# Scan factors of two mixers on VectorE instead of GpSimd, and one weight chunk of the third mixer split earlier

## The chip, the cores and the metric

The kernel runs on one core of a Trainium2 chip. The core has TensorE (matrix products into PSUM banks), VectorE, ScalarE and GpSimd (elementwise work) and SyncE, which only issues loads here. The engines run their own instruction streams in order and meet at semaphores. The metric is the device time of one execution, in microseconds; lower is better.

## The reference, cut to what matters

The model is two blocks in a row on 256 tokens of width 1024, all in float32. The first block (attention, a Fourier mix and a convolutional feed-forward, two layers) is not touched by the change. The second block has two layers, which this text calls the second and the third mixer. Both contain a gated scan over time in chunks of 32 tokens, forwards and backwards:

```python
def _chunk_gated_scan(q, k, v, log_g):
    ...
    b = jnp.cumsum(log_g, axis=2)
    ref = b[:, :, CHUNK // 2 - 1:CHUNK // 2]
    s = jnp.einsum('bnthk,bnshk->bnhts', q * jnp.exp(b - ref), k * jnp.exp(ref - b))
    s = jnp.where(np.tril(np.ones((CHUNK, CHUNK), bool)), s, 0.0)
    o_intra = jnp.einsum('bnhts,bnshv->bnthv', s, v)
    b_last = b[:, :, -1]
    q_dec = q * jnp.exp(b)
    k_dec = k * jnp.exp(b_last[:, :, None] - b)
    ...

def _mixer_c(h, w_in, lower_bounds, layer_idx, norm_gain, w_out):
    proj = jnp.einsum('bsd,df->bsf', h, w_in)
    q, f_f, f_b, i, gate = _split(proj, (C_WIDTH,) * 5)
    ...
    f = lb + (1.0 - lb) * jax.nn.sigmoid(z)        # forget: k = 1 - f, g = log f, per direction
    o = bidirectional_gated_scan(silu(q) * scale, k_f, g_f, k_b, g_b, i)
    y = _head_rmsnorm(o, norm_gain) * jax.nn.silu(gate)
    return y @ w_out
```

## The kernel before, in words

**Products.** Weights come in chunks of 1 MB (128 x 2048 floats) that SyncE loads into a ring of two slots. So that a product keeps float32's accuracy, each chunk is split in two: ScalarE makes the coarse part (`split`, L1055), VectorE the fine part (`fine`, L1627), and TensorE adds three products (L464 to L466). There are two pairs of coarse and fine buffers: a chunk can be split once TensorE has done with the chunk two before it, and its load can start once the fine part of the chunk two before it is made. TensorE writes products in four banks in turn; ScalarE or VectorE read a bank before it is used again.

**The scan.** A scan works on two heads and one direction, as tiles of 128 x 512. It does not step through time: the products of decay factors are arranged so that TensorE gets all scores of 256 tokens at once, in four parts: inside chunks of 32 (L860), between neighbouring chunks (L868), between pairs of chunks (L874, tile `span2`) and between halves of 128 tokens (L881, tile `span3`). Around it, per scan:

- `decays` on VectorE (L2123 to L2140): cumulative sums of the log gates and their differences, and the small sums for the spans.
- `exponentials` on ScalarE (L1422 to L1428): five instructions, in the order inv, last, spans, mid, run, each of which raises `exps_ready`.
- `factors` on VectorE (L2146, L2147, L2153): after the fourth exponential `mid` times q and `inv` times k (`qe_ready`: TensorE may start L860), and then, once GpSimd has made its products, two near factors into `span2`.
- `scan` on GpSimd (L2479, L2481, L2488): `last` times k (`kd_ready`), `run` times q (`qd_ready`), and two far factors into `span3`. This is what VectorE waits for between L2147 and L2153, and TensorE at L868 and L881.

The second mixer makes 4 scans, the third 12: six groups of two heads, each with both directions. GpSimd does nothing else in the two mixers but issue a few small loads.

**A group of the third mixer.** The order is written out by hand on each engine. TensorE takes, in group g: the scores of both directions (L860 to L881), the q product of group g+1, the output of the scan (L895), the value and the output gate's product of group g+1, the sum of squares for the norm (L908), and the two sigmoid products (forget gates) of group g+2. ScalarE turns each product into its activation, with an ACT_TABLE_LOAD where the function changes, and between these makes the coarse parts, the exponentials, and the norm's copy, square and root (L1434, L1436, L1443). VectorE masks the scores (L2167), makes the decays of g+1 with a fine part behind each, the factors of g+1, two fine parts (L1627), the norm (`c_norm`, L2181 to L1641), one more fine part (the q chunk), and the forget gates of g+2 (`forget`, L2315, L2318). The first product of the next group needs that q chunk's fine part and a bank that the first mask has read. In the last two groups the sigmoid products, the forget gates and the later fine parts drop out; in group 4 the first chunk of the output projection stands in the sigmoid chunk's place.

The call `split(CHUNK8, ahead=2)` waits for two more products than ScalarE has already read.

Of the kernel before, what the change touches and what calls it, by code (L numbers as in the profile page):

```python
# [9 lines left out]
ALU = mybir.AluOpType  # L10
# [3 lines left out]
P = 128  # L14
# [183 lines left out]
def two_block_kernel(nc, a, out):  # L198
    ctx = ExitStack()
    with ctx:  # L200
# [797 lines left out]
        def _(act):  # L998
# [50 lines left out]
            def split(size, loads=1, ahead=0):  # L1049

                s, v = ring.next(loads)
                act.wait_ge(landed[s], v)
                act.wait_ge(gemm_done, u.made_now() + ahead)
                p = coarse.n % PAIRS
                nc.scalar.copy(w_co[:, p, 0:size], raw_w[:, s, 0:size]).then_inc(coarse_ready, 1)  # L1055
                coarse.next()
# [373 lines left out]
            def scan_norm(banks, scale):  # L1430
                seen_next(scan_read)
                act.wait_ge(y_ready, seen[y_ready].n)
                for j, ps in enumerate(banks):
                    step(nc.scalar.activation(osb[:, j * 512:(j + 1) * 512], ps[:, :], ACT.Copy, scale=scale))  # L1434
                for j, ps in enumerate(banks):
                    m = nc.scalar.activation(osq[:, j * 512:(j + 1) * 512], ps[:, :], ACT.Square, scale=scale)  # L1436
                    if j < len(banks) - 1:
                        step(m)
                m.then_inc(o_sq, 1)
# [107 lines left out]
            for g in range(C_GROUPS):  # L1547
                more, gates = g + 1 < C_GROUPS, g + 2 < C_GROUPS
                for d in range(2):
                    scan_scores(d)  # L1550
                if more:
                    split(CHUNK8)
                    split(CHUNK8, ahead=2)
                    features_out(ACT.Silu, input_half(g + 1, C_Q))
                    exponentials(0, 1.0)
                    exponentials(1, 1.0)
                else:
                    split(CHUNK8)
                scan_norm([pb[6 + g % 2]], C_DIM ** -0.5)
                if more:  # L1560
                    tokens_out(values(g + 1))
                    split(CHUNK8)
                    features_out(ACT.Silu, out_gate(g + 1))
                scan_root(C_DIM)
                if gates:
                    for d in range(2):
                        features(ACT.Sigmoid, input_half(g + 2, C_K + d))
                    log_gates(g + 2)
# [5 lines left out]
        def _(dve):  # L1574
# [22 lines left out]
            def step(ins):  # L1597

                ins.then_inc(dve_done, 1)
                done.next()  # L1600
# [540 lines left out]

            def factors(d, scan, q, k):

                run, mid, last, inv, span2, _ = decay[d]
                dve.wait_ge(exps_ready, 5 * scan + 4)
                step(nc.vector.tensor_tensor(mid, mid, q, ALU.mult))  # L2146
                nc.vector.tensor_tensor(inv, inv, k, ALU.mult).then_inc(qe_ready, 1)  # L2147
                near = spans[d][:, 0, :].rearrange("p (a c) -> p a c", c=4)
                for src, half in ((last, d), (run, 1 - d)):
                    seen_next(kd_ready if src is last else qd_ready)  # L2150
                    o, i = [v.rearrange("p (a c t) -> p a c t", c=4, t=CHUNK)[:, :, 2 * half:2 * half + 2, :] for v in (span2, src)]
                    by = near[:, :, 2 * half:2 * half + 2].rearrange("p a (c o) -> p a c o", o=1).to_broadcast([P, 2 * GROUP, 2, CHUNK])
                    m = nc.vector.tensor_tensor(o, i, by, ALU.mult)  # L2153
                    if src is last:
                        step(m)
                m.then_inc(span2_ready, 1)

            masked = []

# [164 lines left out]
            def c_factors(g, d):  # L2324
                factors(d, 4 + 2 * g + d, c_in[g % 2][:, C_Q, :], c_in[g % 2][:, C_K + d, :])
# [14 lines left out]
            for g in range(C_GROUPS):  # L2340
                more, gates = g + 1 < C_GROUPS, g + 2 < C_GROUPS
                for d in range(2):
                    scan_scores(d)
                if more:
                    c_decays(g + 1, 0)
                    fine(CHUNK8)
                    c_decays(g + 1, 1)
                    skip(2)
                    fine(CHUNK8)
                    evacuated()  # L2350
                    c_factors(g + 1, 0)
                    c_factors(g + 1, 1)
                    skip(2)
                    fine(CHUNK8)
                    skip(2)
                    root = roots()
                else:
                    fine(CHUNK8)
                    root = roots()
                if gates:  # L2360
                    fine(CHUNK8)
                c_norm(g, root)
                if gates:
                    skip(2)
                    chunk()
                    forget(g + 2)
# [5 lines left out]
        def _(pool):  # L2372
# [97 lines left out]
                pool.dma_start(lnb[:, 0, :], row_bcast(a["ln_gain_2"], l * D, D)).then_inc(ln_loaded, 16)  # L2470
                pool.dma_start(lnb[:, 1, :], row_bcast(a["ln_bias_2"], l * D, D)).then_inc(ln_loaded, 16)
            norm_rows(0)
            n_scans = [0]

            def scan(d, q, k):

                run, _, last, _, _, span3 = decay[d]
                pool.wait_ge(exps_ready, 5 * n_scans[0] + 2)
                nc.gpsimd.tensor_tensor(last, last, k, ALU.mult).then_inc(kd_ready, 1)  # L2479
                pool.wait_ge(exps_ready, 5 * n_scans[0] + 5)  # L2480
                nc.gpsimd.tensor_tensor(run, run, q, ALU.mult).then_inc(qd_ready, 1)  # L2481
                n_scans[0] += 1
                far = spans[d][:, 1, :].rearrange("p (h c) -> p h c", h=GROUP)
                for src, t in ((last, d), (run, 1 - d)):
                    pool.wait_ge(kd_ready if src is last else qd_ready, n_scans[0])
                    o, i = [v.rearrange("p (h c t) -> p h c t", h=GROUP, t=CHUNK)[:, :, 4 * t:4 * t + 4, :] for v in (span3, src)]
                    by = far[:, :, 4 * t:4 * t + 4].rearrange("p h (c o) -> p h c o", o=1).to_broadcast([P, GROUP, 4, CHUNK])
                    m = nc.gpsimd.tensor_tensor(o, i, by, ALU.mult)  # L2488
                    if src is run:
                        m.then_inc(span3_ready, 1)  # L2490
            for grp in range(2):
                for d in range(2):
                    scan(d, *[v[:, 2 * grp:2 * grp + 2, :].rearrange("p h t -> p (h t)") for v in (qbT, kbT)])
            pool.wait_ge(x_done, updates + 2)
            norm_rows(1)
            for g in range(C_GROUPS):
                for d in range(2):
                    scan(d, c_in[g % 2][:, C_Q, :], c_in[g % 2][:, C_K + d, :])
            for t in range(2):
                pool.wait_ge(x_done, updates + 3 + t)  # L2500
                pool.dma_start(out[0, t * P:(t + 1) * P, :], x_tok[:, t, :]).then_inc(out_saved, 16)
# [169 lines left out]
```

## Time and profile before

| | us |
|---|---|
| median of 3 timed runs | 2200.82 |
| lowest, highest | 2198.29, 2203.59 |
| profiled execution | 2197.82 |
| its span | 2196.0 |
| TensorE, busy | 1964.1 (89%) |
| VectorE, busy | 1225.0 (56%) |
| ScalarE, busy | 942.2 (43%) |
| GpSimd, busy | 213.4 (10%) |

The mean granted TensorE clock is 0.944 of full speed. The second mixer's scans lie between 1756 and 1812 us of the span, the third mixer from 1867 to the end. A TensorE product's row gives a modelled end, so products are followed by their starts. In the chain of waits a piece's length is the time until the next piece takes over; in a timeline it is the instruction's own duration, which can overlap the next instruction's start.

### The profile page before, as it was taken

Reading aid. Unit: us, or ns where it says so; the run is one execution under the profiler, and the core shown is the slowest. Engines: PE = TensorE matmul, PEld = TensorE weight load, DVE = VectorE, ACT = ScalarE, POOL = GpSimd, SP = SyncE. Lnnn points to the kernel's source line nnn. Section 1 sums busy time; section 2 is a strip of 40 time slices with the busy share of each in tenths; the row PEclk is TensorE's granted clock in tenths of the full one; section 3 lists DMA queues with packets and bytes.
Section 4 is the critical chain, followed back from the end, with each engine's and each line's share of the span. In section 5 each row is a group of like instructions: output and inputs, shape, how many; then the busy total and the mean of one; then the engine's idle time right before and its main releaser. Section 6 shows DMA issues by size and latency. Waiting matters only on the chain. (4 is left out here: it accounts for less than half of the span.)

```text
span 2196.0 us, 31241 instructions
## 1 busy us (share of the span) xinstructions
PE 1964.1 (89%) x12007; PEld 1646.1 (75%) x12007; DVE 1225.0 (56%) x1841; ACT 942.2 (43%) x1387; POOL 213.4 (10%) x216
## 2 busy tenths in 40 slices
PE   5988899999998999999977999899988967799886
PEld 3864576688877888887844799799887865789885
DVE  3338556343346555423565456677444576678885
ACT  3323444332324444312434555566336452566751
POOL 3000000000000222200000000022100030111310
PEclk9989999999998999999987999899998988899988
DMA  8226546333231222323310056455563323433331
GB/s 287 89 79 218 166 136 216 93 86 107 81 115 58 96 96 96 121 100 105 110 44 1 19 164 182 147 173 173 190 222 108 116 71 103 134 116 120 111 120 73
DMA packets 262663, 265.88 MB, mean 121 GB/s; under 512 B 6278, under 2 KB 230896, under 8 KB 262560
## 3 DMA queue, kind: packets, MB, share of 16 engines
q1 hardware_dynamic: 257008, 247.22, 35.3%
q0 software_dynamic: 4832, 15.06, 2.1%
q10 hardware_dynamic: 720, 2.17, 0.2%
q8 instruction: 71, 1.16, 0.2%
q14 instruction: 32, 0.26, 0.0%
HBM read 263.33 MB, written 1.10 MB: 120 GB/s over the span
## 5 line engine op out<-in xcount | busy, mean ns | idle before, releaser
L1627 DVE TENSOR_TENSOR weights_fine<-region,weights_coarse 128x2048 fp32r<-128x2048 f32 (+3 forms) x187 | 431.9, 2310 | 403.9 <-ACT weights_coarse L1055 403.1
L1055 ACT CAST weights_coarse<-region 128x2048 fp32r<-128x2048 f32 (+3 forms) x187 | 358.9, 1919 | 370.9 <-PE bank L466 353.2
L464 PE MATMUL bank<-normed_coarse,weights_coarse 128*128 128x512 f32 (+1 forms) x1088 | 367.7, 338 | 14.4 <-DVE normed_fine L1733 9.1
L465 PE MATMUL bank<-normed_fine,weights_coarse 128*128 128x512 f32 (+1 forms) x1088 | 366.7, 337 | 0.0
L466 PE MATMUL bank<-normed_coarse,weights_fine 128*128 128x512 f32 (+1 forms) x1088 | 366.6, 337 | 0.0
L464 PEld LDWEIGHTS bank<-normed_coarse,weights_coarse 128*128 128x128 f32 x1088 | 207.5, 191 | 37.8 <-issue 13.6
L465 PEld LDWEIGHTS bank<-normed_fine,weights_coarse 128*128 128x128 f32 x1088 | 207.6, 191 | 21.3
L466 PEld LDWEIGHTS bank<-normed_coarse,weights_fine 128*128 128x128 f32 x1088 | 207.5, 191 | 21.4
L464 PE MATMUL bank<-x_turned_coarse,weights_coarse 128*128 128x256 f32 x616 | 185.3, 301 | 34.4 <-DVE weights_fine L1627 30.4
L465 PE MATMUL bank<-x_turned_fine,weights_coarse 128*128 128x256 f32 x616 | 182.3, 296 | 0.0
L466 PE MATMUL bank<-x_turned_coarse,weights_fine 128*128 128x256 f32 x616 | 181.8, 295 | 0.0
L464 PEld LDWEIGHTS bank<-x_turned_coarse,weights_coarse 128*128 128x128 f32 x616 | 127.0, 206 | 38.4 <-DVE weights_fine L1627 32.8
L458 PE MATMUL bank<-ident,region 128*128 128x128 f32 (+3 forms) x449 | 80.2, 320 | 83.3 <-DVE region L1831 28.7
L458 PEld LDWEIGHTS bank<-ident,region 128*128 128x128 f32 (+3 forms) x449 | 62.1, 166 | 108.7 <-DVE region L1831 35.4
L1306 ACT ACTIVATE region<-bank,cols 128x512 f32<-128x512 f32 (+1 forms) x88 | 59.1, 671 | 196.5 <-PE bank L466 196.5
L465 PEld LDWEIGHTS bank<-x_turned_fine,weights_coarse 128*128 128x128 f32 x616 | 127.0, 206 | 0.0
L466 PEld LDWEIGHTS bank<-x_turned_coarse,weights_fine 128*128 128x128 f32 x616 | 126.4, 205 | 0.0
L1981 DVE SCALAR_TENSOR_TENSOR region<-bank,cols,region 128x510 f32<-128x510 f32 (+1 forms) x88 | 54.0, 614 | 113.5 <-ACT region L1306 112.9
L665 PE MATMUL bank<-region 96*128 96x512 f32 (+4 forms) x224 | 106.0, 564 | 7.4 <-ACT region L1393 4.4
L464 PE MATMUL bank<-weights_coarse,ffn_mid_coarse 128*128 128x512 f32 x264 | 102.8, 390 | 0.9 <-DVE region L1954 0.9
L465 PE MATMUL bank<-weights_fine,ffn_mid_coarse 128*128 128x512 f32 x264 | 102.7, 389 | 0.0
L466 PE MATMUL bank<-weights_coarse,ffn_mid_fine 128*128 128x512 f32 x264 | 102.7, 389 | 0.0
(265 smaller groups left out, 3781.0 us busy)
## 6 DMA issues: line engine op xcount, KB each, us to landing
region<-in_w_mod SPq DMA_DIRECT2D x48, 1024.0 KB, 5.1
region<-in_w_up SPq DMA_DIRECT2D x44, 1024.0 KB, 4.9
region<-in_w_in_c SPq DMA_DIRECT2D x30, 1024.0 KB, 5.0
region<-in_w_in_ab SPq DMA_DIRECT2D x20, 1024.0 KB, 5.1
region<-in_w_in SPq DMA_DIRECT2D x32, 512.0 KB, 4.3
region<-in_w_down SPq DMA_DIRECT2D x16, 1024.0 KB, 4.9
region<-in_w_in SPq DMA_DIRECT2D x14, 1024.0 KB, 5.0
region<-in_w_in SPq DMA_DIRECT2D x16, 384.0 KB, 3.4
```

The source lines that it names most:

```text
L458: mm = nc.tensor.transpose(ps[0:w, j * width:j * width + parts_in], blk, ident[0:parts_in, 0:parts_in])
L464: nc.tensor.matmul(o, sc, mc, start=first, stop=False)
L465: nc.tensor.matmul(o, sc, mf, start=False, stop=False)
L466: return nc.tensor.matmul(o, sf, mc, start=False, stop=last)
L665: nc.tensor.matmul(pb[4 + J % 2][:, 0:keys_of(i)[1] * P], q, k, start=True, stop=True).then_inc(scores_done, 1)
L1055: nc.scalar.copy(w_co[:, p, 0:size], raw_w[:, s, 0:size]).then_inc(coarse_ready, 1)
L1306: nc.scalar.activation(acc[:, j, 0:n], ps[:, 0:n], ACT.Identity, scale=cols[:, 2 * l, bass.ds(c + T_TAP1, 1)], bias=cols[:, 2 * l + 1, bas ...
L1627: nc.vector.tensor_tensor(w_fi[:, p, 0:size], raw_w[:, s, 0:size], w_co[:, p, 0:size].bitcast(F32), ALU.subtract).then_inc(fine_ready, 1)
L1981: link(nc.vector.scalar_tensor_tensor(out=a_s[:, :, 1:SEQ], in0=u_s[:, :, 0:SEQ - 1], scalar=cols[:, 2 * l, bass.ds(f + T_TAP0, 1)], in1=a ...
```

## The change

Two things are done. First, all of GpSimd's `scan` goes into VectorE's `factors`. A factor block now has eight instructions instead of four, in the order last times k, mid times q, inv times k, run times q, two near, two far factors; TensorE's first wait (`qe_ready`) is raised by the third instead of the second. This holds for all 16 scans. Second, in the third mixer's groups 0 to 4, ScalarE makes the coarse part of the first sigmoid chunk (for group 4: of the first output chunk) before the norm's copy and square and not after the value copies; and VectorE makes its fine part between the factors of direction 0 and those of direction 1 instead of after both.

```diff
@@ ScalarE, third mixer, group g
+                if more:
+                    split(CHUNK8, ahead=2)
                 scan_norm([pb[6 + g % 2]], C_DIM ** -0.5)
                 if more:
                     tokens_out(values(g + 1))
-                    split(CHUNK8)
                     features_out(ACT.Silu, out_gate(g + 1))
@@ VectorE
             def factors(d, scan, q, k):
-                run, mid, last, inv, span2, _ = decay[d]
+                run, mid, last, inv, span2, span3 = decay[d]
                 dve.wait_ge(exps_ready, 5 * scan + 4)
+                nc.vector.tensor_tensor(last, last, k, ALU.mult).then_inc(kd_ready, 1)
                 step(nc.vector.tensor_tensor(mid, mid, q, ALU.mult))
                 nc.vector.tensor_tensor(inv, inv, k, ALU.mult).then_inc(qe_ready, 1)
+                dve.wait_ge(exps_ready, 5 * scan + 5)
+                nc.vector.tensor_tensor(run, run, q, ALU.mult).then_inc(qd_ready, 1)
                 near = spans[d][:, 0, :].rearrange("p (a c) -> p a c", c=4)
+                far = spans[d][:, 1, :].rearrange("p (h c) -> p h c", h=GROUP)
...
                 m.then_inc(span2_ready, 1)
+                for src, t in ((last, d), (run, 1 - d)):
+                    o, i = [v.rearrange("p (h c t) -> p h c t", h=GROUP, t=CHUNK)[:, :, 4 * t:4 * t + 4, :] for v in (span3, src)]
+                    by = far[:, :, 4 * t:4 * t + 4].rearrange("p h (c o) -> p h c o", o=1).to_broadcast([P, GROUP, 4, CHUNK])
+                    m = nc.vector.tensor_tensor(o, i, by, ALU.mult)
+                    if src is last:
+                        step(m)
+                m.then_inc(span3_ready, 1)
@@ VectorE, third mixer, group g
                     c_factors(g + 1, 0)
+                    fine(CHUNK8)
                     c_factors(g + 1, 1)
-                    skip(2)
-                    fine(CHUNK8)
-                    skip(2)
+                    skip(4)
@@ GpSimd
-            def scan(d, q, k):
...
-            for grp in range(2):
-                for d in range(2):
-                    scan(d, *[v[:, 2 * grp:2 * grp + 2, :].rearrange("p h t -> p (h t)") for v in (qbT, kbT)])
             pool.wait_ge(x_done, updates + 2)
             norm_rows(1)
-            for g in range(C_GROUPS):
-                for d in range(2):
-                    scan(d, c_in[g % 2][:, C_Q, :], c_in[g % 2][:, C_K + d, :])
```

VectorE before, in a group of the third mixer, from the second decays' fine part on. L2146, L2147 and the pair L2153 are one direction's factors; L2181 is the norm's reciprocal:

```order
L1627 TENSOR_TENSOR weights_fine<-region,weights_coarse 128x2048
L2146 TENSOR_TENSOR region<-region 128x512
L2147 TENSOR_TENSOR region<-region 128x512
L2153 TENSOR_TENSOR region<-region 128x4x64 x2
L2146 TENSOR_TENSOR region<-region 128x512
L2147 TENSOR_TENSOR region<-region 128x512
L2153 TENSOR_TENSOR region<-region 128x4x64 x2
L1627 TENSOR_TENSOR weights_fine<-region,weights_coarse 128x2048 x2
L2181 RECIPROCAL region<-region 128x512
```

The same place on VectorE now, by the changed file's lines (one line lower, L1628 for the fine part; L2147 last times k, L2148 mid times q, L2149 inv times k, L2151 run times q, L2158 near, L2165 far factors):

```order
L1628 TENSOR_TENSOR weights_fine<-region,weights_coarse 128x2048
L2147 TENSOR_TENSOR region<-region 128x512
L2148 TENSOR_TENSOR region<-region 128x512
L2149 TENSOR_TENSOR region<-region 128x512
L2151 TENSOR_TENSOR region<-region 128x512
L2158 TENSOR_TENSOR region<-region 128x4x64 x2
L2165 TENSOR_TENSOR region<-region 128x2x128 x2
L1628 TENSOR_TENSOR weights_fine<-region,weights_coarse 128x2048
L2147 TENSOR_TENSOR region<-region 128x512
L2148 TENSOR_TENSOR region<-region 128x512
L2149 TENSOR_TENSOR region<-region 128x512
L2151 TENSOR_TENSOR region<-region 128x512
```

Of the two fine parts that stood behind both blocks, one has moved between them; each block has become longer by two 128x512 and two 128x256 instructions.

ScalarE in the same group, as a difference. L1426 and L1428 are the last two exponentials, L1434 and L1436 the norm's copy and square, L1047 the value product's copies, L1393 the output gate's activation:

```order
 L1426 ACTIVATE region<-region 128x512
 L1428 ACTIVATE region<-region 128x512
+L1055 CAST weights_coarse<-region 128x2048
 L1434 ACTIVATE region<-bank 128x512
 L1436 ACTIVATE region<-bank 128x512
 L1047 COPY region<-bank 128x256 x2
-L1055 CAST weights_coarse<-region 128x2048
 L1393 ACT_TABLE_LOAD
 L1393 ACTIVATE region<-bank 128x256 x2
```

The coarse part has moved ahead of four short instructions; what follows keeps its order. TensorE's and SyncE's orders are the same in both kernels.

## Rows read from the trace of the kernel before

**Rows 1.** Waits, 1840 to 2180: waiter <- releaser: us in total, times, longest us.

```profile
PE bank L464 <- DVE weights_fine L1627: 29.1, 6, 8.9
```

**Rows 2.** Chain that ended last, 1740 to 2196: start us, us, what.

```profile
1943.35 0.53 ACT region L1426
1944.01 1.15 DVE region L2146
1945.16 1.71 DVE region L2147
1946.86 1.51 DVE region L2153 x2
1948.38 1.71 DVE region L2146
...
1953.27 2.21 DVE weights_fine L1627
...
2116.99 0.53 ACT region L1426
...
2129.12 3.27 DVE region L2181
```

**Rows 3.** By line: count, duration ns min/median/max, first and last start.

```profile
L2147 DVE TENSOR_TENSOR region<-region x16: 685/1756/1784, 1762.9 to 2123.6; 128x512 f32<-128x512 f32 x16
...
L2153 DVE TENSOR_TENSOR region<-region x32: 413/832/1492, 1764.6 to 2126.1; 128x256 f32<-128x256 f32 x32
...
L2479 POOL TENSOR_TENSOR region<-region x16: 1262/1300/1482, 1761.2 to 2121.7; 128x512 f32<-128x512 f32 x16
```

**Rows 4.** Timeline of VectorE: start us, us, engine, line, op, out<-in, [idle before <-releaser].

```profile
1904.00 0.69 DVE L2147 TENSOR_TENSOR region<-region 128x512 f32<-128x512 f32 x1
```

**Rows 5.** Windows: us, busy (xcount) of PE PEld DVE ACT POOL, clock, DMA, GB/s.

```profile
1955.50:1960.70 5.20, 5.18 (x24) 5.18 (x25) 5.01 (x2) 1.44 (x2) 0.00 (x0) 0.50 0.81 267
...
1960.90:1966.50 5.60, 5.60 (x49) 5.60 (x49) 3.40 (x7) 2.56 (x3) 0.00 (x0) 1.00 0.32 113
```

**Rows 6.** Timeline of the group whose first product starts at 1930.80, three engines.

```profile
1946.50 0.58 ACT L1434 ACTIVATE region<-bank 128x512 f32<-128x512 f32 x1
...
1953.77 1.89 ACT L1055 CAST weights_coarse<-region 128x2048 fp32r<-128x2048 f32 x1
...
1955.52 0.58 PE L464 MATMUL bank<-x_turned_coarse,weights_coarse 128*128 128x256 f32 x1 [4.56 <-DVE weights_fine L1627]
...
1957.90 3.34 DVE L2181 RECIPROCAL region<-region 128x512 f32<-128x512 f32 x1
...
1966.14 2.29 DVE L1627 TENSOR_TENSOR weights_fine<-region,weights_coarse 128x2048 fp32r<-128x2048 f32 x1 [2.06 <-ACT weights_coarse L1055]
...
1969.49 1.05 PE L860 MATMUL bank<-region 128*128 128x128 f32 x8
...
1970.28 0.73 DVE L2315 TENSOR_SCALAR region<-region,lbv 128x256 f32<-128x256 f32 x2 [1.85 <-ACT region L1393]
...
1972.50 0.73 DVE L2167 COPY_PREDICATED region<-tri,bank 128x512 f32<-128x512 uint32 x1
...
1974.45 0.36 PE L464 MATMUL bank<-x_turned_coarse,weights_coarse 128*128 128x256 f32 x1
```

**Rows 7.** Timeline of the last scan of the second mixer.

```profile
1795.86 1.22 DVE L2146 TENSOR_TENSOR region<-region 128x512 f32<-128x512 f32 x1 [1.85 <-ACT region L1426]
...
1798.81 2.07 PE L860 MATMUL bank<-region 128*128 128x128 f32 x8 [8.30 <-DVE region L2147]
```

**Rows 8.** Timeline of VectorE at the third mixer's start, and one decays block.

```profile
1897.45 1.21 DVE L2125 TENSOR_TENSOR_SCAN region<-region 128x512 f32<-128x512 f32 x1
...
1910.13 4.48 DVE L1627 TENSOR_TENSOR weights_fine<-region,weights_coarse 128x2048 fp32r<-128x2048 f32 x2
...
1936.28 1.22 DVE L2125 TENSOR_TENSOR_SCAN region<-region 128x512 f32<-128x512 f32 x1
...
1939.24 2.28 DVE L1627 TENSOR_TENSOR weights_fine<-region,weights_coarse 128x2048 fp32r<-128x2048 f32 x1
```

More of the change, by code:

```diff
@@ L2472, in _ @@
             norm_rows(0)
-            n_scans = [0]
-            def scan(d, q, k):
[L2477 to L2490, printed above, removed]
-            for grp in range(2):
-                for d in range(2):
-                    scan(d, *[v[:, 2 * grp:2 * grp + 2, :].rearrange("p h t -> p (h t)") for v in (qbT, kbT)])
             pool.wait_ge(x_done, updates + 2)
             norm_rows(1)
-            for g in range(C_GROUPS):
-                for d in range(2):
-                    scan(d, c_in[g % 2][:, C_Q, :], c_in[g % 2][:, C_K + d, :])
             for t in range(2):
```

## The prediction, made before the changed kernel was run

> **What bounds the kernel now.** I read the times and the page's first line first: the profiled execution took 2197.82 us around a span of 2196.0 us, and the median of the timed runs is 2200.82 us, 3.0 us above it; I sum against the profiled execution and add the 3.0 us at the end. Measurement of this kernel cannot tell less than about 0.2% (4.4 us) from no change.
>
> The change touches only the second and third mixer, so I read the waits there. In the third mixer TensorE is waited on by nothing for long except once per group: its product stands for the fine part of a weight chunk, 29.1 us in 6 waits [rows 1]. The chain of waits says what is late there [rows 2]: ScalarE's fourth exponential (1943.35), then VectorE with six factor instructions of direction 0 and 1 from 1944.01 to 1953.27, then the fine part (2.21 us), and only then TensorE. The same stretch returns in every group, at 1943.35 and at 2116.99 four groups later, so a period is (2116.99 - 1943.35) / 4 = 43.41 us. The reader should see in rows 2 that the multiplications last 1.7 us each, and in rows 3 that this is not their own length: the same instruction has a minimum of 685 ns and a median of 1756 ns. GpSimd multiplies in the same microseconds, at a median of 1300 ns (last row there). Where VectorE had the machine to itself it took 0.69 us [rows 4].
>
> **The cost of one factor block on VectorE.** Before: from 1944.01 to 1948.38, 4.4 us, for two 128x512 and two 128x256 multiplications [rows 2]. Now: four of 128x512 and four of 128x256, with GpSimd silent. The nearest uncontended durations are 0.69 us [rows 4] and 0.41 us, the minimum in rows 3, second row. Summed as they stand that is 4 x 0.69 + 4 x 0.41 = 4.4 us; but consecutive instructions overlap by about 0.08 us (the chain gives the fine part 2.21 us from its start to the next, rows 2, where its own row has 2.28, rows 8), so I take 3.9 us. Two of the narrow ones (the far factors, 128x2x128) the trace shows on GpSimd alone. The nearest rows are the near factors of equal size, 0.41 us alone and 1.49 us at most [rows 3], so the block lies between 3.9 and 3.9 + 2 x 1.1 = 6.1 us, and nothing excludes a few tenths below; I take 3.9, since the slow end belongs to contention.
>
> The Trainium skill weighs against moving work this way: "Perfetto Trace Analysis", section Optimizing Scalar/DVE Operations, says that when VectorE is saturated, handing work to GpSimd may help, though it adds that the two share a read port and so it might not. By its first half the change adds about 1.9 us to each of 16 blocks, some 30 us of VectorE; by its second half, it adds none. Rows 3 and 4 side with the second half.
>
> **A group of the third mixer, step by step** [rows 6]. Direction 0's block runs from 1944.01 to 1947.9. ScalarE is free of exponentials at 1946.50, where the norm's copy now starts; instead it makes the coarse part of the first sigmoid chunk, 1.9 us, until 1948.4. VectorE waits 0.5 us for it and has the fine part done at 1950.65. TensorE ran dry at 1955.52 - 4.56 = 1950.96, so that wait goes. With it goes the low clock: right after the wait 24 matmuls took 5.2 us at a granted clock of 0.50 (1.2 GHz), against 49 in 5.6 us at 1.00 (2.4 GHz) shortly after [rows 5]. 24 at full clock take 2.8 us, so 2.4 us more. TensorE alone would be about 6.9 us earlier.
>
> What is late next: ScalarE's total work up to the second sigmoid split is only reordered, so that split still starts at 1953.77. VectorE's direction 1 block ends at 1950.65 + 3.9 = 1954.55, inside this cover, with 1.1 us to spare; the second fine part ends at 1957.90 as before, and the reciprocal starts there as before. TensorE starts the second product at 1957.9 instead of 1969.49 - 5.8 = 1963.7 (5.8 us: rival 2). VectorE ends the norm at 1966.14 - 2.06 = 1964.1; the following fine part no longer waits (2.06 us) and ends at 1966.3; the forget gates no longer wait (1.85 us) and start at 1966.3 instead of 1970.28. From there to the first mask is 2.2 us, so the mask starts at 1968.5 instead of 1972.50. The mask, 0.7 us, frees the bank of the next group's first product: 1969.2 instead of 1974.45. The product was to begin 43.65 us after the last group's, at the start given in the heading of rows 6, so the group becomes 38.4 us long. ScalarE to 1955.7 and then VectorE bind it, no longer TensorE's wait. Against the mean period of 43.41 that is 5.0 us, four times: 20.1 us. The moved chunk's load is released by a fine part two chunks earlier, which does not move against it; TensorE's queue order and all loads keep theirs.
>
> **The other terms.** In the last group with factors two blocks and one fine part take 3.9 + 0.5 + 2.2 + 3.9 = 10.5 us instead of 2129.12 - (2116.99 + 0.66) = 11.5 us, 1.0 us less; I count 0.8. At the mixer's start [rows 8] VectorE's decays take 1939.24 - 1936.28 = 2.96 us alone; from 1897.45 they would end at 1900.4, two blocks at 1908.2, against 1910.13: 1.9 us less. In the second mixer [rows 7] TensorE begins its scores after two multiplications, 2.95 us after the block's start; now after three, 3 x 0.61 + 0.05 = 1.9 us, 1.05 us less in the first and fourth scan. There the added first multiplication stands ahead of what TensorE waits for, and still it gains. In the middle two the block's end leads to a fine part and the gain is 4.4 - 3.9 = 0.5 us each. That makes 3.1 us; I count 3.0, as the first scan's shift may be absorbed in part. GpSimd's 16 scans leave its queue; only DMA issues that wait for later events remain, no term.
>
> Sum: 20.1 + 0.8 + 1.9 + 3.0 = 25.8 us. 2197.82 - 25.8 = 2172.0, and with the 3.0 us 2175.0 us.
>
> **Rivals.**
> 1. *The early split stands.* At 1946.50 the split needs its chunk landed and the value product done. At its old place, 1.5 us later, it showed no wait, which bounds the delay: if it lost all 1.5 us, the norm's copies, the root and the second split would come 1.5 us late, the whole period with them. Then 4 x 3.5 + 5.7 = 19.7 us, 2181. Against it: the load had some 5 us of silence. Chance 0.12.
> 2. *The clock still falls.* TensorE now has a wait near 1956.8 to 1957.9 instead. Should that bring the low clock, the second product is 2.4 us longer; A product takes (1969.49 - 1955.52 - 2.4) / 2 = 5.8 us at full clock and the scores 1974.45 - 1969.49 = 5.0 us [rows 6], so TensorE would reach the next product at 1957.9 + 5.8 + 2.4 + 5.0 = 1971.1, not 1969.2. Four times 1.9 us: 2183. For it: rows 5 show how one wait cost it. Against it: this one is a quarter as long. Chance 0.07.
> 3. *TensorE's own work sets the period.* If VectorE's end of the group is quicker than I think, the period falls to TensorE's sum, about 43.65 - 4.56 - 2.4 = 36.7 us; 4 x 6.7 + 5.7 = 32.5 us, 2168. Chance 0.10.
> 4. *The multiplications are slow by themselves*, whoever else works (their operands, not GpSimd). Then a block is 4 x 1.7 + 4 x 0.76 = 9.8 us. The second fine part of a group ends at 1944.01 + 9.8 + 2.2 + 9.8 + 2.2 = 1968.0, 10.1 us late; the next product starts at 1979.3, 4.9 us later than before, four times; last group +10.3, start +9.9, second mixer 2 x 2.2 + 2 x 5.4. Sum +55 us, 2256. It decides from a block of 7.4 us, where the loop gains nothing. For it: 1.7 us is the common value; against it rows 4 and the minima of rows 3. Chance 0.03.
> 5. *The change does little*: TensorE's wait only moves to the second fine part. For it: that fine part keeps its time. Then only the other terms' 5.7 us would be left: 2195, at the edge of what cannot be told. Against it: both idle times of VectorE after it were waits for TensorE's products. Chance 0.03.
>
> The Trainium skill ("SBUF — State Buffer", section Who interferes with whom) makes the contention an exclusive lock between a VectorE instruction with two SBUF inputs and a GpSimd one that reads SBUF. If instead the two shared a rate, or rival 4 held, the 1.7 us would shrink less or not at all; rows 3 and 4 agree with the lock.
>
> **How the numbers follow.** My forecast, 2175, has 0.65, with its own range 2170 to 2180. Rivals 1 and 2 reach to 2187 with their spread, rival 3 to 2167: range 2167 to 2187, leaving out rivals 4 and 5 and a little. Faster by over 0.2%: 0.95; within 0.2%: 0.02; slower: 0.03.
>
> **What would show it.** VectorE's 128x512 multiplications at 0.69 us throughout; blocks near 3.9 us; no wait of TensorE for a fine part longer than 1.5 us in the third mixer's loop, and no stretch at 0.50 there; the period 38.4 us; ScalarE's first exponentials of successive groups that far apart; scores of the second mixer 1.9 us after their block's start. Blocks above 5 us, idle time of ScalarE ahead of the moved split, or a period above 40 us would make it wrong.

## The result, and the profile after

The changed kernel takes **2174.34 us** (median of 4 runs, 2171.61 to 2176.02) against 2201.84 us (2198.29 to 2203.59) for the kernel before, run beside it: ratio 0.9876, interval 0.9859 to 0.9893. That is 27.5 us less. Forecast were 2175.0 us, 0.7 us more, and a gain of 25.8 us.

The profiled execution has a span of 2174.2 us. The page's first part, busy time and instruction count by engine, next to the table of before: VectorE got 64 more instructions, and its busy time fell, from 1225.0 us.

```profile
PE 1961.4 (90%) x12007; PEld 1639.7 (75%) x12007; DVE 1211.8 (56%) x1905; ACT 941.6 (43%) x1387; POOL 136.3 (6%) x152
```

The changed kernel by source line (count, duration ns min/median/max, first and last start), answering to [rows 3]: the 128x512 multiplication `last` times k and the 128x256 far factors. The median is now within 10 ns of the minimum.

```profile
L2147 DVE TENSOR_TENSOR region<-region x16: 682/692/694, 1767.1 to 2105.4; 128x512 f32<-128x512 f32 x16
...
L2165 DVE TENSOR_TENSOR region<-region x32: 410/416/419, 1770.2 to 2108.9; 128x256 f32<-128x256 f32 x32
```

Its waits from 1830 to 2160, answering to [rows 1] (29.1 us in 6 waits, 8.9 at most):

```profile
PE bank L464 <- DVE weights_fine L1628: 13.6, 6, 6.6
PE bank L895 <- DVE region L2179: 6.1, 1, 6.1
```

Its chain of waits (start us, us, what), answering to [rows 2]:

```profile
1944.33 0.52 ACT region L1426
...
1946.96 0.62 ACT region L1428
1947.57 1.79 ACT weights_coarse L1055
...
1954.84 1.80 ACT weights_coarse L1055
1956.66 2.29 DVE weights_fine L1628
1958.95 3.27 DVE region L2193
...
1967.16 0.74 DVE region L2327 x2
...
1969.38 0.73 DVE region L2179
...
2098.15 0.52 ACT region L1426
...
2109.26 3.27 DVE region L2193
...
2165.97 0.53 POOL out L2488
```

No factor instruction is left in a group's chain: it now runs along ScalarE to its second split (1954.84), then the fine part, the reciprocal (L2193), the forget gates, the mask. The same exponential returns at 1944.33 and, four groups later, at 2098.15: the period is 153.82 / 4 = 38.46 us instead of 43.41.

Its timeline (start us, us, engine, line, op, out<-in, [idle before <-releaser]), answering to [rows 6 to 8]:

```profile
1767.07 0.69 DVE L2147 TENSOR_TENSOR region<-region 128x512 f32<-128x512 f32 x1 [1.85 <-ACT region L1426]
...
1799.59 0.69 DVE L2147 TENSOR_TENSOR region<-region 128x512 f32<-128x512 f32 x1 [1.85 <-ACT region L1426]
...
1801.54 2.08 PE L860 MATMUL bank<-region 128*128 128x128 f32 x8 [6.89 <-DVE region L2149]
...
1912.56 0.58 PE L464 MATMUL bank<-x_turned_coarse,weights_coarse 128*128 128x256 f32 x1 [6.64 <-DVE weights_fine L1628]
...
1944.98 0.69 DVE L2147 TENSOR_TENSOR region<-region 128x512 f32<-128x512 f32 x1 [2.48 <-ACT region L1426]
...
1949.40 2.29 DVE L1628 TENSOR_TENSOR weights_fine<-region,weights_coarse 128x2048 fp32r<-128x2048 f32 x1 [0.57 <-ACT weights_coarse L1055]
...
1951.74 0.38 PE L464 MATMUL bank<-x_turned_coarse,weights_coarse 128*128 128x256 f32 x1
...
1956.66 2.29 DVE L1628 TENSOR_TENSOR weights_fine<-region,weights_coarse 128x2048 fp32r<-128x2048 f32 x1 [1.23 <-ACT weights_coarse L1055]
...
1959.01 0.38 PE L464 MATMUL bank<-x_turned_coarse,weights_coarse 128*128 128x256 f32 x1 [1.26 <-DVE weights_fine L1628]
...
1964.96 2.28 DVE L1628 TENSOR_TENSOR weights_fine<-region,weights_coarse 128x2048 fp32r<-128x2048 f32 x1
...
1970.25 0.36 PE L464 MATMUL bank<-x_turned_coarse,weights_coarse 128*128 128x256 f32 x1 [0.19 <-DVE region L2179]
...
2116.94 3.48 PE L895 MATMUL bank<-region 128*128 128x128 f32 x16 [6.14 <-DVE region L2179]
```

TensorE stands at 1951.74 without a wait, where it had waited 4.56 us, and has 1.26 us at 1959.01. The clock is seen in windows (us, busy and count of PE, PEld, DVE, ACT, POOL, clock, DMA share, GB/s), of the changed kernel:

```profile
1912.50:1919.10 6.60, 6.54 (x32) 6.54 (x33) 2.21 (x2) 0.38 (x1) 0.00 (x0) 0.54 0.86 292
1951.70:1957.70 6.00, 6.00 (x50) 5.80 (x48) 4.77 (x9) 5.94 (x7) 0.00 (x0) 1.00 0.55 178
1959.00:1965.00 6.00, 5.99 (x50) 5.99 (x51) 5.86 (x7) 1.77 (x2) 0.00 (x0) 1.00 0.53 175
2116.90:2122.80 5.90, 4.68 (x21) 4.38 (x22) 2.11 (x1) 1.11 (x3) 0.00 (x0) 0.74 0.47 135
```

and of the kernel before, at the places that answer to the first and the last of these:

```profile
1912.40:1919.00 6.60, 6.53 (x39) 6.53 (x40) 2.22 (x2) 0.65 (x2) 0.00 (x0) 0.69 0.84 288
2136.80:2143.80 7.00, 5.83 (x21) 5.17 (x22) 2.06 (x1) 1.08 (x2) 0.00 (x0) 0.50 0.40 150
```

Both of the group's sigmoid products run at 1.00 (2.4 GHz); [rows 5] had 0.50 (1.2 GHz).

**The account.** The profiled execution of the changed kernel reaches the first factors 5.3 us later than that of before (1767.07 against 1761.74), although the instructions ahead of them are the same; over the profiled executions of this study that place lies between 1760.8 and 1769.6 by the first `mid` exponential. So I compare from there: to the last output transfer it is 2165.97 - 1767.07 = 398.9 us instead of 2187.77 - 1761.74 = 426.0. The difference, 27.1 us, agrees with the 27.5 of the medians; that of the spans (21.8) would mislead.

The ends of the stretches in the kernel before, by its timeline and the end of its chain (those of the changed kernel stand above):

```profile
1761.74 1.22 DVE L2146 TENSOR_TENSOR region<-region 128x512 f32<-128x512 f32 x1 [1.85 <-ACT region L1426]
...
1912.47 0.58 PE L464 MATMUL bank<-x_turned_coarse,weights_coarse 128*128 128x256 f32 x1 [8.87 <-DVE weights_fine L1627]
```

```profile
2187.77 0.53 POOL out L2501
```

| Stretch (us) | before | after | change | forecast |
|---|---|---|---|---|
| second mixer, first block to the last scan's scores | 37.07 | 34.47 | -2.6 | -3.0 |
| from there to the third mixer's first decays | 93.47 | 93.06 | -0.4 | 0 |
| mixer's start to its first sigmoid product | 20.19 | 17.96 | -2.2 | -1.9 |
| that product to the loop's first factors | 31.54 | 32.42 | +0.9 | 0 |
| four periods | 173.64 | 153.84 | -19.8 | -20.1 |
| last group, first block to reciprocal | 11.48 | 10.46 | -1.0 | -0.8 |
| reciprocal to the end | 58.65 | 56.71 | -1.9 | 0 |

Part of what the mixer's start gained lies ahead of its factors. In the kernel before, GpSimd's multiplications met VectorE's decays there too; a 128x512 subtraction of the decays in its timeline:

```profile
1898.70 1.73 DVE L2129 TENSOR_TENSOR region<-region 128x512 f32<-128x512 f32 x1
```

In the changed kernel the same subtraction (L2130, at 1901.02) lasts 0.69 us.

### The profile page after: what moved, and what is told of

It reads as the page before. It is cut to its first block and busy times, and to the rows that moved or that the text cites. A ratio compares the mean times of both kernels' runs of the same rounds, so it can differ in the third digit from the quotient of the medians.

```text
span 2174.2 us, 31241 instructions
## 1 busy us (share of the span) xinstructions
PE 1961.4 (90%) x12007; PEld 1639.7 (75%) x12007; DVE 1211.8 (56%) x1905; ACT 941.6 (43%) x1387; POOL 136.3 (6%) x152
## 5 line engine op out<-in xcount | busy, mean ns | idle before, releaser
L1628 DVE TENSOR_TENSOR weights_fine<-region,weights_coarse 128x2048 fp32r<-128x2048 f32 (+3 forms) x187 | 431.9, 2310 | 403.0 <-ACT weights_coarse L1055 402.2
L464 PE MATMUL bank<-x_turned_coarse,weights_coarse 128*128 128x256 f32 x616 | 182.2, 296 | 19.1 <-DVE weights_fine L1628 14.3
```

The source lines that it names most:

```text
L464: nc.tensor.matmul(o, sc, mc, start=first, stop=False)
L1628: nc.vector.tensor_tensor(w_fi[:, p, 0:size], raw_w[:, s, 0:size], w_co[:, p, 0:size].bitcast(F32), ALU.subtract).then_inc(fine_ready, 1)
```

## The experiments

"Anchored" is the span less the start of the first `mid` exponential: 434.9 us before, 407.8 after. The period is read from the loop's exponentials. Ratios are to the kernel before, run beside each.

**Which half does what.** Two kernels with one half of the change each. Factors on VectorE, the split where it was:

```diff
-if more:
-    split(CHUNK8, ahead=2)
 scan_norm([pb[6 + g % 2]], C_DIM ** -0.5)
 if more:
     tokens_out(values(g + 1))
+    split(CHUNK8)
...
 c_factors(g + 1, 0)
-fine(CHUNK8)
 c_factors(g + 1, 1)
-skip(4)
+skip(2)
+fine(CHUNK8)
+skip(2)
```

> All scan factors on VectorE, but the sigmoid chunk's coarse and fine part stay where they were. My theory: the two parts of the change remove the same wait, so they do not add up. Blocks are 3.75 us, the fine part starts 1.7 us earlier than before in a group, and TensorE still waits about 3 us there; the loop gains 1.7 us a group if the low clock still follows that wait and 4 us if not. With 5 us from the second mixer and the third's start: 2179 to 2189 us. Rival, contention is the whole story: 2174 to 2177 us.

Measured 2186.51 us (2183.12 to 2190.38), ratio 0.9933 (0.9921 to 0.9946), inside the 2179 to 2189 of the theory and outside the rival's 2174 to 2177. The period is 40.94. Its timeline and the window behind the wait:

```profile
1951.93 0.58 PE L464 MATMUL bank<-x_turned_coarse,weights_coarse 128*128 128x256 f32 x1 [2.88 <-DVE weights_fine L1627]
```

```profile
1951.90:1957.00 5.10, 5.07 (x31) 5.07 (x32) 3.24 (x2) 3.49 (x4) 0.00 (x0) 0.70 0.64 206
```

The blocks are short, but the fine part still stands behind two of them: TensorE waits 2.88 us in each group, and part of the stretch behind it runs at the low clock. The other half, GpSimd keeping its factors (ScalarE and VectorE in the order of the change):

> The sigmoid chunk's split moved, GpSimd keeps its factors. My theory: the first fine part can start behind one contended block (4.4 us), TensorE's wait shrinks to 1 us or less, ScalarE and then VectorE set the same period of about 38.5 us. The loop gains nearly all, the second mixer and the start nothing: 2178 to 2182 us. Rival, the parts add up: this one gives the 27.5 us less what the factors alone give, 2186 to 2194 us.

Measured 2180.20 us (2179.75 to 2184.45), ratio 0.9908 (0.9893 to 0.9922), period 38.47: the whole gain of the loop, and inside the theory's 2178 to 2182. Timeline, VectorE and GpSimd:

```profile
1952.21 3.26 DVE L1628 TENSOR_TENSOR weights_fine<-region,weights_coarse 128x2048 fp32r<-128x2048 f32 x1
...
1951.84 1.48 POOL L2479 TENSOR_TENSOR region<-region 128x512 f32<-128x512 f32 x1
1953.28 3.33 POOL L2481 TENSOR_TENSOR region<-region 128x512 f32<-128x512 f32 x1
```

The fine part is held up too, 3.26 us instead of 2.29. It reads as taking turns: GpSimd's first instruction ends at 1953.32, and the fine part ends 2.15 us later, at 1955.47, about its own length; GpSimd's next, begun at 1953.28, needs 3.33 us where its median is 1.75, and ends 1.14 us after the fine part. Yet the period does not grow: ScalarE's run to the second split covers it.

So the halves overlap. Against 2202.15 us of that batch the factors alone give 15.6 us, the split alone 22.0, together 27.5 and not 37.6. In the loop they give 2.5, 4.9 and, together, 4.95 us a group. What the factors add to the split, 2180.20 - 2174.34 = 5.9 us by the medians, lies outside the loop. By the traces it lies at two places: in the second mixer the split alone needs as long as the kernel before (37.71 us from the first `mid` exponential to the last scan's scores, in both; 35.12 in the changed kernel), and from the third mixer's first decays to its first sigmoid product too (20.18 and 20.19; 17.96). That makes 2.6 + 2.2 = 4.8 us.

**What slows VectorE.** To the changed kernel I add work on GpSimd beside the factors, into an unused tile: multiplications of the same count and sizes that GpSimd made before, reading constants, and then, for the rival that any activity of GpSimd costs, fills that read nothing.

```diff
+for words in (512, 512, 256, 256):      # first kernel, per scan; waits left out
+    nc.gpsimd.tensor_tensor(spare[:, 0:words], resets[:, 0:words], resets[:, 0:words], ALU.mult)
...
+for _ in range(8):                      # second kernel, per scan
+    nc.gpsimd.memset(spare, 0.0)
```

> The changed kernel, and GpSimd makes as many multiplications of the old sizes as it used to, of constants into a spare tile that nobody reads. My theory, that the two engines exclude each other: VectorE's 128x512 multiplications are at 1.7 us again where GpSimd runs, a block of direction 0 takes about 7 us, the period grows by 3 to 4 us: 2190 to 2205 us. Rival, the long durations came from waiting for GpSimd's results and not from its running: blocks stay at 3.75 us, 2174 us.

Measured 2207.36 us (2202.89 to 2215.66), ratio 1.0033 (1.002 to 1.0046), period 42.04: the whole gain is gone, and a little more. The period grew by 3.6 us, as expected (3 to 4); the time lies above the expected 2190 to 2205. Anchored it is 438.9 us, 31.1 more than the changed kernel: 14.3 in the four periods, 11.1 ahead of the loop and 5.7 behind its last exponential, places that the expectation did not count. Timeline:

```profile
1955.68 0.96 DVE L2149 TENSOR_TENSOR region<-region 128x512 f32<-128x512 f32 x1 [2.48 <-ACT region L1428]
1956.56 1.52 DVE L2150 TENSOR_TENSOR region<-region 128x512 f32<-128x512 f32 x1
...
1955.05 8.66 POOL L2491 TENSOR_TENSOR region<-region 128x512 f32<-128x512 f32 x8 [37.80 <-ACT region L1426]
```

A block takes 1963.91 - 1955.68 = 8.2 us instead of 3.75 (7 were expected). The multiplications read constants and nobody reads what they make, so waiting for GpSimd's results, the rival, is excluded.

> The changed kernel, and GpSimd fills the same spare tile eight times per scan, which only writes. If the exclusion concerns only what GpSimd reads, VectorE's multiplications stay at 0.69 us and the time at 2174 us. If any work of GpSimd excludes VectorE, they rise as in the kernel with multiplications, 2180 us or more.

Measured 2173.96 us (2171.24 to 2176.60), ratio 0.9885 (0.9869 to 0.9902), period 38.47, as without the fills. Timeline of GpSimd, and the line of the multiplication beside it:

```profile
1939.54 9.29 POOL L2491 MEMSET region<- 128x512 f32 x16 [34.18 <-ACT region L1426]
```

```profile
L2149 DVE TENSOR_TENSOR region<-region x16: 683/692/695, 1762.5 to 2100.7; 128x512 f32<-128x512 f32 x16
```

GpSimd works from 1939.54 to 1948.83, beside direction 0's block (from 1940.19), the fine part behind it (2.29 us, unchanged) and the first half of direction 1's block, and costs them nothing. It is its reading that holds up VectorE's two-input instructions, not its running. The Trainium skill ("SBUF — State Buffer", section Who interferes with whom) states it so: two inputs in SBUF contend with a GpSimd instruction that reads SBUF, not with one that only writes; these two traces agree.

**How much cover is there?** One, and then six, more 128x512 multiplications on VectorE, behind direction 1's block in each group; the forecast had 1.1 us to spare there.

```diff
 c_factors(g + 1, 1)
+for _ in range(N):         # N = 1, then 6
+    link(nc.vector.tensor_tensor(spare, resets, resets, ALU.mult))
```

> The changed kernel with one more 128x512 multiplication at the end of direction 1's block in groups 0 to 4, 0.7 us. My theory: VectorE has 1.2 us to spare there before the second fine part, so it costs nothing in groups 0 to 3 and 0.7 us in group 4: 2175 us. Rival, VectorE binds: 5 x 0.7 = 3.5 us, 2178 us.

The period is 38.54, 0.08 us more; timeline:

```profile
1956.79 2.29 DVE L1629 TENSOR_TENSOR weights_fine<-region,weights_coarse 128x2048 fp32r<-128x2048 f32 x1 [0.69 <-ACT weights_coarse L1056]
```

VectorE's wait shrinks from 1.23 to 0.69 us, and the period takes almost nothing: it is cover. The time, 2178.99 us (2170.07 to 2179.69), ratio 0.9891 (0.9866 to 0.9917), does not separate the theories: its interval holds the changed kernel's ratio. In the profiled execution the excess lies in the tail (from the last group's exponential at 2098.46 to the end 79.0 us instead of 76.1), where a window is at the low clock throughout:

```profile
2115.00:2122.00 7.00, 3.75 (x16) 3.49 (x16) 4.93 (x6) 0.14 (x1) 0.00 (x0) 0.50 0.09 8
```

Of the 2.9 us, 0.7 are the added multiplication ahead of the reciprocal in group 4. The other 2.2 are not its doing: from group 4's reciprocal to the last output transfer it is 58.97 us here, and 58.70 in the kernel with a second moved split (below), which has no added multiplication, against 56.79 in the changed kernel.

> The same with six more, 4.1 us. My theory: 1.2 us of it are covered, 2.9 us come through in each of four groups, and all 4.1 us in group 4: 15.7 us, 2190 us. Rival, nothing is covered: 20.5 us, 2195 us; rival, TensorE has slack behind it: under 8 us, below 2182 us.

Measured 2196.79 us (2193.87 to 2201.45), ratio 0.9982 (0.9969 to 0.9994), period 43.06: 4.6 us more, where 2.9 were expected. By time alone this is the rival's value (nothing is covered, 2195 us), and not the theory's 2190; the timeline has to decide. It and the window:

```profile
1951.31 4.32 DVE L2368 TENSOR_TENSOR region<-region 128x512 f32<-128x512 f32 x6
...
1958.00 0.39 PE L465 MATMUL bank<-x_turned_coarse,weights_coarse 128*128 128x256 f32 x1 [4.30 <-DVE weights_fine L1629]
```

```profile
1958.00:1963.00 5.00, 5.00 (x29) 5.00 (x30) 4.90 (x5) 0.33 (x1) 0.00 (x0) 0.66 0.63 210
```

The second fine part starts 1955.65 - 1940.93 = 14.72 us behind the group's first factors, against 1956.66 - 1944.98 = 11.68: of 4.1 us added 3.0 come through, so the cover is real. The wait for that fine part is 4.30 us, 3.0 more, and with it the low clock returns: 29 matmuls in 5.0 us, 59 in the next 5.0, at 1.00. That is the term that my expectation lacked; it is what is left of the 4.6 us, 1.6.

**What binds the loop now.** ScalarE's run to its second split stands in the chain. Here its coarse part goes ahead of the output gate's activation, saving the table load and activation in front of it:

```diff
 tokens_out(values(g + 1))
+if gates:
+    split(CHUNK8, ahead=2)
 features_out(ACT.Silu, out_gate(g + 1))
```

> The changed kernel with the coarse part of the second sigmoid chunk ahead of the output gate's activation on ScalarE. My theory: ScalarE's run of work until that split is what binds a group, and TensorE's 1.25 us wait for the second fine part shows it. The wait goes, the period falls from 38.4 to 37.2 us, 4 x 1.25 = 5 us: 2169 us. Rival, VectorE's work behind it or the norm's root, now 1.9 us later, binds: no gain, 2174 us.

Measured 2170.41 us (2167.24 to 2172.24), ratio 0.986 (0.9846 to 0.9875), period 37.15 against 37.2 expected. The coarse part now starts 3.69 us after the moved one (1942.00), not 7.26:

```profile
1945.69 1.91 ACT L1055 CAST weights_coarse<-region 128x2048 fp32r<-128x2048 f32 x1 [0.31 <-PE bank L466]
```

The run of ScalarE did bind. To this I add that the norm's second half goes behind the next decays' fine part, and `mid` and `inv` are multiplied before `last`, so that TensorE's scores wait for two instructions, not three:

```diff
-nc.vector.tensor_tensor(last, last, k, ALU.mult).then_inc(kd_ready, 1)
 step(nc.vector.tensor_tensor(mid, mid, q, ALU.mult))
 nc.vector.tensor_tensor(inv, inv, k, ALU.mult).then_inc(qe_ready, 1)
+nc.vector.tensor_tensor(last, last, k, ALU.mult).then_inc(kd_ready, 1)
...
-c_norm(g, root)
+norm_root(root); late.append(g)     # norm_rest behind the next fine part
```

> The same, and VectorE puts the second half of the norm behind the next group's first decays, and a block starts with the two multiplications TensorE waits for. My theory: nothing but TensorE's own products binds a group then, 36.6 us; 4 x 1.85 = 7.4 us, and 0.6 us in each of two scans of the second mixer: 2166 us. Rival, the postponed half makes a fine part late for TensorE: 2169 to 2174 us.

Measured 2168.59 us (2164.78 to 2174.70), ratio 0.9852 (0.9834 to 0.9871), period 36.98 (36.6 expected), anchored 400.4 against 404.6. The theory said 2166 us, its rival 2169 to 2174, and by time alone it is told apart from neither, nor from the kernel before it. The period is near 36.7 us, the forecast's sum of TensorE's own work (rival 3).

**The long wait at the mixer's start.** The awaited chunk's coarse part goes between the two scans' exponentials, the fine parts ahead of and between the blocks:

```diff
 exponentials(0, 1.0)
+split(CHUNK8)
 exponentials(1, 1.0)
-features(ACT.Silu, out_gate(0))
+features_out(ACT.Silu, out_gate(0))
...
 c_decays(0, 1)
+chunk()
 c_factors(0, 0)
+chunk()
 c_factors(0, 1)
-for _ in range(3):
-    chunk()
+chunk()
```

> The version of before (second split early, half of the norm late, waited-for multiplications first), and at the third mixer's start the chunk that TensorE waits 6.6 us for is split between the two directions' exponentials, with its fine part ahead of both factor blocks and the next one between them. My theory: that wait is VectorE's order alone, some 6 us of it and 2 to 3 us of low clock behind it go: 2160 us. Rival, the load of that chunk or the next fine part is late, and half comes back as another wait: 2164 to 2167 us.

Measured 2161.85 us (2158.50 to 2165.36), ratio 0.9811 (0.9796 to 0.9825); 2160 were expected. The wait of 6.64 us is gone whole. The only wait for a fine part that is left ahead of the loop is one of 1.95 us before an earlier product, and it stood in the changed kernel too (second row):

```profile
1900.95 0.39 PE L464 MATMUL bank<-x_turned_coarse,weights_coarse 128*128 128x256 f32 x1 [1.95 <-DVE weights_fine L1631]
```

```profile
1899.90 0.39 PE L464 MATMUL bank<-x_turned_coarse,weights_coarse 128*128 128x256 f32 x1 [1.95 <-DVE weights_fine L1628]
```

**The tail.** The last group's mask waits behind the norm of the group before. Here the norm of group 4 goes ahead of the last fine part:

```diff
 else:
+    c_norm(g - 1, root)
     fine(CHUNK8)
...
-else:
+elif not more:
     c_norm(g, root)
```

> The same, and VectorE masks the last group's scores ahead of the norm of the group before it, for which TensorE waits 6.1 us. My theory: the scan's output then is ready when that norm ends, the 3.6 us of the output matmuls leave the chain and less low clock follows: 2155 to 2157 us. Rival, the last norm's chain is hidden behind the output projection: 2160 us.

Measured 2159.11 us (2156.07 to 2162.97), ratio 0.9801 (0.9785 to 0.9818), the lowest median of all. It misses the expected 2155 to 2157 and is nearer to the rival's 2160. Timeline:

```profile
2097.06 2.02 PE L895 MATMUL bank<-region 128*128 128x128 f32 x16 [0.67 <-ACT region L1411]
2103.86 2.08 PE L908 MATMUL bank<-region 128*128 128x256 f32 x4 [4.78 <-ACT region L1436]
```

The wait for the mask, 5.93 us in the kernel before it in this series (6.14 in the changed kernel), became 0.67, but the one before the next product, for the norm's square, grew from 1.17 to 4.78: of 5.3 us won 3.6 came back. The 2.7 us between the two medians are less than each kernel's own spread, so that this step gains anything is not shown.

## Why the prediction was right

- **A block of 3.9 us.** It was 1906.47 - 1902.72 = 3.75 us, at the mixer's start, where the next block follows at once (those two starts are by VectorE's timeline). The far factors, seen on GpSimd only, took 0.42 us as their nearest row [rows 3] said, and the upper bound of 6.1 was not needed. Rival 4 (slow by themselves) is refuted by the unchanged instruction (`inv` times k, L2149 now) at a median of 684 ns, and its counterpart, contention, is shown by the reading and the writing kernel. The forecast also said that rows 3 and 4 agree with a lock rather than with a shared rate. They do not decide that: with GpSimd silent both give 0.69 us. What speaks for turns is the timeline of the kernel with the split alone. And the rows from 1944.01 to 1953.27 hold eight factor instructions, not the six that it counted; its cost of a block used the right four.
- **The group.** The executions differ by 0.97 us at its first factors (1944.01, 1944.98). With that added, the forecast's second fine part ends at 1958.87: the reciprocal started at 1958.87. The fine part behind the norm was to end at 1967.3, and the forget gates started at 1967.16; the next product was to start at 1970.2, and did at 1970.25. Period 38.46 for 38.4.
- **Rival 1**, the early split waits for its chunk: coarse part at 1947.57 directly behind the last exponential, no wait. **Rival 2**, the clock falls at the second product: the wait was 1.26 us, and the window behind it is at 1.00. The kernel with six extra multiplications shows that its mechanism is real from a longer wait on. **Rival 3**, TensorE binds: not here; with the loop's later versions at 36.98 us it nearly does. **Rival 5**: both idle times went, as argued.
- **Second mixer, 3.0 us.** 2.6 measured; from the block's start to the scores in the last scan 2.95 became 1801.54 - 1799.59 = 1.95 us.
- **Mixer's start, 1.9 us.** 2.2 measured up to the waiting product (the 0.3 more is two blocks of 3.75 and not 3.9), but 0.9 came back at once. The wait fell from 8.87 to 6.64 us, and yet the low clock reached further into the work: in 6.6 us 32 matmuls at 0.54 instead of 39 at 0.69. The forecast gave this product's start no clock term. The change does not force that loss: the kernel with the factors alone has the same instructions there and a wait of 6.65 us, and this window:

```profile
1911.00:1917.60 6.60, 6.57 (x44) 6.57 (x45) 2.18 (x1) 0.38 (x1) 0.00 (x0) 0.78 0.86 293
```
- **The tail, counted as nothing, gave 1.9 us, and that looks like luck.** TensorE's wait for the last mask is 6.14 instead of 7.16 us, and behind it the clock is 0.74 instead of 0.50 on average. But the kernel with the second moved split has the same instructions from there on and the same wait of 6.14 us, and it went through the low clock like the kernel before:

```profile
2106.20:2113.20 7.00, 5.79 (x21) 5.15 (x22) 2.11 (x1) 1.08 (x2) 0.00 (x0) 0.50 0.48 150
```

From group 4's reciprocal (2098.48) to its last output transfer (2157.18) it took 58.70 us; by the same rows it is 58.73 before and 56.79 after. So both values occur with the changed tail, and what chooses between them stays open.

So three terms had no forecast, -0.4, +0.9 and -1.9; they add up to -1.4 us, about what 27.1 us exceeds 25.8 by. None of the three is shown to come from the change: the stretch of -0.4 is 92.12 us in the kernel with the split alone and 93.47 before, with the same instructions, and for the other two see above. The four terms that had a forecast gave 25.6 us for its 25.8; the 1.7 us between the forecast and the medians' 27.5 are no more than such differences between executions. The mechanism and the large terms held: the period and each place in the group came out within 0.2 us of the working.

What the forecast did not say is how the two halves divide the gain. It worked them out together, and a reader may take the short multiplications for the source of the loop's gain. The split alone gives all of it; the factors give the same microseconds again, in part, and their own 4.8 us (traces) to 5.9 us (medians) elsewhere.

## What to carry to other kernels

If an instruction's minimum by line is well under its median, look at what another engine does in the same microseconds before taking the median for its cost; moving that work back can lower the busy time of the engine that receives it. Price a moved piece by the chain that remains: two edits that remove the same wait are worth the larger one. Add the clock to the price of each wait of TensorE that appears, and to the gain of each that goes, from windows behind waits at that place, and from more than one execution: what two microseconds of one trace are due to is only known when a second trace with the same instructions has them too.

## What the runs showed of the hardware

- GpSimd's reading stretched VectorE's two-input instructions: 128x512 from 0.69 us to between 0.96 and 1.78 [rows 3], the 128x2048 subtraction from 2.29 to 3.26, a whole block from 3.75 to 8.2. Fills by GpSimd over 9.3 us left the blocks beside them at 0.69 and the subtraction at 2.29.
- At the mixer's start a 128x4 copy, which has one input, took 0.59 us in the kernel before (L2137 at 1902.62) and 0.16 in the changed one. Whether it was held up itself or stood behind the instruction ahead of it, no run separates.
- The hold-up went both ways: GpSimd's multiplication took 3.33 us instead of its median 1.75 when it met the subtraction.
- Behind waits of 1.26 us, TensorE's clock was 1.00; behind 2.88 us, 0.70 over 5.1 us; behind 4.30 us, 0.66 over 5.0 us. At the mixer's start a wait of 6.64 us had 0.54 behind it in one execution and one of 6.65 us 0.78 in another, with the same instructions, and one of 8.87 us 0.69, all over 6.6 us. In the tail 6.14 us had 0.74 over 5.9 us or 0.50 over 7.0 us behind them. So the wait's length alone does not set how far the low clock reaches. What else does stays open here.
